# Two blocks in one kernel: one expert of 64 places to a bin with a floating 17th bin in the two later expert layers, and stage boundaries taken tile by tile

## The chip, the cores and the metric

The kernel runs on one core of one Trainium2 chip. The metric is the device time of one launch in microseconds (us), the median of several runs. PE is the matmul engine (TensorE), DVE the VectorE, ACT the ScalarE, POOL the GpSimd; SP issues nearly all the large transfers. All numbers are float32.

## What is computed

The reference is two blocks in a row on 256 tokens of width 1024. The first block has a mixer layer with a dense feed-forward part, then a convolution layer with 8 experts of which each token takes 2. The second block has two layers; each ends in 16 experts, of which a token takes 2 inside one group of 4:

```python
def grouped_moe(x, router_w, router_b, w_gate, w_up, w_down):
    ...
    scores = jax.nn.sigmoid(jnp.dot(xt.astype(jnp.float32), router_w.astype(jnp.float32)))
    sel = scores + router_b.astype(jnp.float32)
    group_score = lax.top_k(sel.reshape(-1, N_GROUPS, GROUP_SIZE), TOP_K)[0].sum(-1)
    top_group = jnp.argmax(group_score, axis=-1)
    ...
    for e in range(N_EXPERTS_2):
        h = jax.nn.silu(xt @ w_gate[e]) * (xt @ w_up[e])
        out = out + combine[:, e:e + 1] * (h @ w_down[e])
    return out.reshape(bsz, seq, d)
...
def second_block(...):
    for i in range(DEPTH):
        ...
        x = layer_norm(ALPHA * x + o, ln1_g[i], ln1_b[i])
        f = grouped_moe(x, router_w, router_b, w_gate[i], w_up[i], w_down[i])
        x = layer_norm(ALPHA * x + f, ln2_g[i], ln2_b[i])
```

Here d = 1024 and an expert is 512 wide, so the three weight matrices of one expert are 6.29 MB and those of one layer's 16 experts 100.7 MB. Between the stages of the first block stand updates `x + gate * rmsnorm(y)`, each followed by a new rmsnorm.

On the inputs that the reference draws, its own router gives the 16 experts of each later layer 5 to 67 tokens: expert 12 has 67 in both layers, the next fullest 55 and 56. The four groups have 47 to 82 tokens.

## The kernel before

The program is written by engine: each engine's stream is fixed in the source, and semaphores tie them. No scheduler reorders anything.

**Three expert stages.** They are objects of a class `Moe`: MOE1 (8 experts, 11 column steps of 256), MOEA and MOEB (the two later layers). A stage sorts tokens into bins of CAP = 96 places. In MOE1 a bin is one expert. In MOEA and MOEB a bin is one group of 4 experts, and the 96 places of the bin are sent through all 4 of its experts; the gate of an expert, zero for places that didn't choose it, is multiplied into the hidden values. A *block* is one column step of one expert: 2.1 MB of up weights (w1 and w3) and 1.05 MB of down weights. MOE1 has 88 blocks, MOEA and MOEB 32 each (16 experts by 2 steps).

**A round** on PE is `up(r)` (L1080): the array is used as four column strips of 32, each strip takes 32 places of some block, so a block of 96 places is three strips, a round four, and a stage has blocks x 3 / 4 rounds (24 in MOEA and MOEB). Each round is 32 matmuls; a float32 matmul shows as two records in the trace, so 64. Then come `turn_hidden` (L1092: two transposes), and `down` (L1108: 12 matmuls, 24 records, per block) for the blocks that were ended two rounds before. Per bin there is one `turn_places` (L1130) and four `scatter` matmuls (L1140), each added by DVE to TOK (L2433). Transposed places and scattered sums go through one PSUM bank, bank 3.

**Ahead of the rounds** the tokens are gathered into the bins by matmuls with one-hot matrices (L1053, one-hots made by DVE at L2365), and in MOEA and MOEB `slot_gates` (L1062) fetches the gates of the places. PE starts to gather once DVE has read the counts (memset of L2372, which frees the bank).

**Loads.** `expert_loads` on SP fills a ring of 4 slots (`ring`, one block's w1 and w3 each, L506) and one of 4 down slots (`dring`, L514). A slot is free when the round that used it is over. Up weights come in pieces of 256 columns, that is 1 KB in a row; down weights 4 KB in a row.

**Boundaries of stages.** `post` takes the statistics of a result (DVE, `bn_stats`), multiplies it by the gate vector GP, waits for ACT's square root (`root`), and updates X; `rms` takes the statistics of X, again a root, and `scale_rows` writes the normed tokens. PE then transposes all 16 pieces (`turn_job`, L777), and ACT copies them (L1440, L1442). Behind the second block's layers `layer_norm` (L1920) does both in one go. PE is given small jobs on the modulation weights to do meanwhile: lists FILL, GAP2 (four jobs before the dense part), GAP3, LATE, GAP4, GAP5. A job's columns are summed (L730), taken by ACT (`mod_parts`, L1471), and turned (L743, L746); DVE reads the outcome (L1992, L1997). For gated columns DVE also needs rows that POOL loads into the one buffer RB (`gate_rows`).

Of the kernel before, what the change touches and what calls it, by code (L numbers as in the profile page):

```python
# [7 lines left out]
P = 128  # L8
F32 = mybir.dt.float32
ALU = mybir.AluOpType  # L10
# [34 lines left out]
class Moe:  # L45
# [3 lines left out]
    def __init__(self, name, bins, experts, halves):  # L49
        self.name, self.bins, self.experts, self.halves = name, bins, experts, halves  # L50
        self.steps = experts * halves
        self.blocks = bins * self.steps
        self.rounds = self.blocks * 3 // 4
        self.before = {}

    def counts(self):

        n = {name: self.rounds for name in ("upped", "silued", "hidden", "turned_h", "hidden_turned")}
        n |= {name: KC * self.bins // 4 for name in ("gathered", "gather_taken")}
        n |= {name: self.bins for name in ("places_turned", "places_taken", "ys_ready", "slots_placed")}  # L60
        n |= {name: 4 * self.bins for name in ("scattered", "added")}
        n |= {name: int(self.experts > 1) for name in ("slot_gated", "slot_gates_taken", "mixed_gates")}
        n |= {"all_placed": TT, "down_done": self.blocks, "up_in": 32 * self.blocks // RING, "down_in": 16 * self.blocks // RING}
        return n

    def pieces(self, r):

        return [divmod(4 * r + g, 3) for g in range(4)]

    def home(self, i, c):  # L70

        return divmod(3 * i + c, 4)

    def done_in(self, i):

        return (3 * i + 2) // 4
# [8 lines left out]
    def starts(self, b):  # L85

        return 3 * b * self.steps // 4
# [3 lines left out]
MOE1 = Moe("1", NE1, 1, NSTEP)  # L91
MOEA = Moe("A", NG, GS, NSTEP2)
MOEB = Moe("B", NG, GS, NSTEP2)
# [46 lines left out]
GAP2 = ["mod0_10", "mod0_11", "mod1_3", "mod1_0"]  # L140
GAP3 = ["mod1_1", "mod1_2"]
# [3 lines left out]
GAP5 = ["mod1_10", "mod1_11"]  # L145
MODS = FILL + GAP2 + GAP3 + LATE + GAP4 + GAP5
# [47 lines left out]
def two_blocks(nc, A, out):  # L194
# [3 lines left out]
    with ExitStack() as ctx:  # L198
# [50 lines left out]
        chosen = sb("chosen", [P, TT, NE1])  # L249
        place = sb("place", [P, TT, NE1 + 1])  # L250
        sgt = sb("sgt", [P, NG, 3, GS])
        sgm = sb("sgm", [P, NG, 2])
# [3 lines left out]
        flag = sb("flag", [P, 4], mybir.dt.int32)  # L256
# [3 lines left out]

        dring = carve(dreg, 0, RING, 2, D)
# [25 lines left out]
        gG = H[0:GR, :, :].rearrange("p a n -> p (a n)")  # L287
        nM = HT[0:GR, 0, :, :].rearrange("p a n -> p (a n)")
# [11 lines left out]
        XGS = {"1": carve(wide, 2 * D, KC, NE1 * CAP), "A": carve(wide, D, KC, NG * CAP), "B": carve(wide, D, KC, NG * CAP)}  # L300
        XG2 = carve(wide, 2 * D, KC, P)
        PMG = arena[:, 4096:4096 + 1536]
        router_parts = H[:, 0, :]
# [3 lines left out]
        PTM = carve(T2f, D + 4 * P, 4, P)  # L307
        PM2 = carve(T2f, D, 2, P)
# [83 lines left out]
        def unrolled(m):  # L392
            return 1 if m is MOE1 else m.halves

# [7 lines left out]
        def second_pass(eng, m, first, steps, tail, end=False):  # L402
# [6 lines left out]
            with eng.If(spilled(eng, m) > 0):  # L409
                with eng.Fori(0, m.bins) as b:  # L410
# [7 lines left out]
                if end:  # L418
                    eng.wait_ge(sem(f"baton{m.name}"), 1 + 2 * m.bins * baton_bin(m))
# [3 lines left out]
        def _(sp):  # L423
# [66 lines left out]
            def expert_loads(m, w1, w3, w2, updated):  # L490


                def columns(i):
                    b, q = divmod(i, m.steps)
                    e, st = divmod(q, m.halves)
                    return b * m.experts + e, slice(st * FSTEP, (st + 1) * FSTEP)

                def up(i):
                    s = i % RING
                    e, f = columns(i)  # L500
                    if i < RING:
                        slot_free(s)
# [14 lines left out]
                for i in range(RING):  # L517
                    up(i)
# [2104 lines left out]
```

## Time and profile before

| | us |
|---|---|
| median of 3 runs | 2550.6 (2549.83 to 2553.07) |
| the profiled execution, its own time | 2545.95 |
| its span, first to last instruction | 2544.2 |
| PE busy | 2360.1 (93%) |
| DVE busy, ACT busy | 487.6 (19%), 366.0 (14%) |
| moved by DMA | 644.55 MB, mean 253 GB/s |

PE rows are records of pipelined matmuls: on four strips at once, 64 records of 0.59 us each take 7 us together. The idle time that a timeline row names stands before that row, with what ended it. "x" is a count. PEld are weight loads, which run beside matmuls.

### The profile page before, as it was taken

The numbers are of one execution on the slowest core, as the hardware profiler recorded it, in microseconds if no ns is written. First come the engines' busy times: TensorE is split into PE (matmuls) and PEld (weight loads), VectorE is DVE, ScalarE is ACT, GpSimd is POOL, SyncE is SP. The second block draws the span as 40 slices with busy tenths as digits, with TensorE's granted clock in tenths as the row PEclk, the third lists the DMA queues.
The fourth block names the chain that finished last, engine by engine and source line by source line (L and its number), as shares of the span: only waits on it lengthen the run. The fifth ranks groups of instructions, "written<-read, shape, count | busy, mean of one in ns | idle before, by whom it ended". The sixth has DMA issues, their size and how long they took to land. (4 is left out here: it accounts for less than half of the span.)

```text
span 2544.2 us, 34498 instructions
## 1 busy us (share of the span) xinstructions
PE 2360.1 (93%) x15206; PEld 1002.0 (39%) x15206; DVE 487.6 (19%) x1168; ACT 366.0 (14%) x868; POOL 33.0 (1%) x78
## 2 busy tenths in 40 slices
PE   4999989998999899999999999886999989799997
PEld 1574634443865332222223222253422227342222
DVE  2143830002094300000000000213100021310002
ACT  2023420001232210000000000121100011110000
POOL 2000000000000000000000000000000000000000
PEclk9999989999999999999999999997999999899999
DMA  8231286444354799999999999812899972479993
GB/s 292 77 122 66 100 286 228 152 141 176 117 207 166 265 316 351 366 364 367 364 366 366 363 364 367 287 64 99 293 364 364 359 274 76 129 244 364 365 359 145
DMA packets 446103, 644.55 MB, mean 253 GB/s; under 512 B 10723, under 2 KB 345019, under 8 KB 445947
## 3 DMA queue, kind: packets, MB, share of 16 engines
q1 hardware_dynamic: 442011, 629.55, 72.0%
q0 software_dynamic: 3936, 12.69, 1.5%
q8 instruction: 126, 2.06, 0.3%
q14 instruction: 30, 0.25, 0.0%
HBM read 641.15 MB, written 1.05 MB: 252 GB/s over the span
## 5 line engine op out<-in xcount | busy, mean ns | idle before, releaser
L1080 PE MATMUL bank<-ring,wide 128*32 128x512 f32 x7296 | 808.2, 595 | 1.7 <-ACT wide L1663 0.9
L1080 PEld LDWEIGHTS bank<-ring,wide 128*32 128x32 f32 x7296 | 231.8, 110 | 548.6 <-issue 548.5
L1108 PE MATMUL bank<-dreg,RB 128*32 128x512 f32 x3648 | 415.0, 595 | 0.0
L1670 ACT ACTIVATE SG<-bank 128x256 f32<-128x256 f32 x114 | 43.7, 383 | 1187.2 <-PE bank L1080 1187.2
L1108 PEld LDWEIGHTS bank<-dreg,RB 128*32 128x32 f32 x3648 | 106.8, 109 | 223.8 <-issue 223.8
L719 PE MATMUL bank<-wide,ring 128*128 128x256 f32 x832 | 182.1, 381 | 0.0
L719 PEld LDWEIGHTS bank<-wide,ring 128*128 128x128 f32 x832 | 158.9, 191 | 23.0 <-issue 1.4
L2409 DVE TENSOR_TENSOR H<-SG,bank 128x256 f32<-128x256 f32 x66 | 27.8, 421 | 717.3 <-ACT SG L1670 717.3
L1007 PE MATMUL bank<-ring,wide 128*128 128x512 f32 x352 | 156.2, 597 | 4.4 <-DVE MODX L1997 4.4
L709 PE MATMUL bank<-ring,wide 128*128 128x512 f32 x352 | 155.2, 599 | 1.0 <-DMA ring<-in_w_kv 1.0
L709 PE MATMUL bank<-ring,T 128*128 128x512 f32 x256 | 113.4, 603 | 1.4 <-ACT sm L1842 0.8
L709 PEld LDWEIGHTS bank<-ring,wide 128*128 128x128 f32 x352 | 67.2, 193 | 82.7 <-issue 81.1
L1007 PEld LDWEIGHTS bank<-ring,wide 128*128 128x128 f32 x352 | 65.9, 192 | 79.8 <-issue 75.0
L2414 DVE SCALAR_TENSOR_TENSOR H<-SG,sgt,bank 128x256 f32<-128x256 f32 x32 | 15.4, 481 | 339.7 <-ACT SG L1670 339.7
L1018 PE MATMUL bank<-dreg,HT 128*128 128x512 f32 x176 | 79.3, 593 | 1.0 <-ACT HT L1623 1.0
L709 PEld LDWEIGHTS bank<-ring,T 128*128 128x128 f32 x256 | 49.2, 194 | 62.5 <-issue 60.3
L1140 PE MATMUL bank<-T 128*128 128x512 f32 x128 | 69.5, 636 | 3.9 <-ACT T L1687 3.9
L2306 DVE SCALAR_TENSOR_TENSOR T<-dreg,PCOL,T 128x256 f32<-128x256 f32 x180 | 71.8, 481 | 0.1
L730 PE MATMUL bank<-ring,CB 128*32 128x512 f32 x384 | 50.3, 655 | 22.3 <-DMA ring<-in_l_mod_w 22.3
L1092 PEld LDWEIGHTS bank<-ident,H 128*128 128x128 f32 x228 | 23.0, 141 | 94.9 <-issue 94.9
L2433 DVE TENSOR_TENSOR TOK<-bank,TOK 128x512 f32<-128x512 f32 x64 | 43.9, 685 | 41.6 <-PE bank L1140 41.6
L2262 DVE TENSOR_TENSOR H<-SG,bank 128x256 f32<-128x256 f32 x22 | 9.2, 420 | 214.0 <-ACT SG L1616 214.0
(388 smaller groups left out, 1403.0 us busy)
## 6 DMA issues: line engine op xcount, KB each, us to landing
ring<-in_l_moe_w SPq DMA_DIRECT2D x176, 1024.0 KB, 11.5
dreg<-in_l_moe_w SPq DMA_DIRECT2D x88, 1024.0 KB, 12.4
ring<-in_w_gate SPq DMA_DIRECT2D x64, 1024.0 KB, 11.3
ring<-in_w_up SPq DMA_DIRECT2D x64, 1024.0 KB, 13.5
dreg<-in_w_down SPq DMA_DIRECT2D x64, 1024.0 KB, 12.2
ring<-in_l_mod_w SPq DMA_DIRECT2D x24, 2048.0 KB, 8.0
ring<-in_l_ffn_w SPq DMA_DIRECT2D x22, 1024.0 KB, 10.1
ring<-in_l_w_in SPq DMA_DIRECT2D x7, 2048.0 KB, 9.0
```

The lines of the kernel that those rows point to most:

```text
L709: m = pe.matmul(o[:, lo:lo + n], src[:, k, t * P:(t + 1) * P], w[:, k, 0:n], start=k == 0, stop=k == KC - 1)
L719: m = pe.matmul(o[:, i * T:(i + 1) * T], w[:, k, (2 * j + i) * P:(2 * j + i + 1) * P], src[:, k, :], start=k == 0, stop=k == KC - 1)
L730: m = pe.matmul(o[QUAD * g:QUAD * (g + 1), :], CQ[:, 4 * r + g, :], w[:, 4 * r + g, :], start=r == 0, stop=r == 1)
L1007: m = pe.matmul(banks[t][:, :], T1[:, k, t * P:(t + 1) * P], ring[:, s, k, :], start=k == 0, stop=k == KC - 1)
L1018: m = pe.matmul(banks[4 + 2 * t + n][:, :], HT[:, t, j, :], dring[:, s, j, n * NCH:(n + 1) * NCH], start=st == 0 and j == 0, stop=st == NS ...
L1080: mm = pe.matmul(banks[r % 2][32 * g:32 * g + 32, :], xg[:, k, at:at + 32], ring[:, i % RING, k, :], start=k == 0, stop=k == KC - 1)
L1108: return pe.matmul(banks[4 + 2 * (b % 2) + h][32 * g:32 * g + 32, :], HQ[:, r % 4, j, 32 * q:32 * q + 32], dring[:, i % RING, j, h * NCH:( ...
L1140: pe.matmul(o[:, :], PTM[:, 2 * h + t, :], YS[:, h * NCH:(h + 1) * NCH], start=True, stop=True).then_inc(sem("moe_scattered"), 1)
L1670: act.activation(SG[:, r % 2, :], banks[r % 2][:, 0:FSTEP], ACT.Silu).then_inc(sem("moe_silued"), 1)
L2306: dve.scalar_tensor_tensor(T2[:, k, :], hT[:, k, tap:tap + T], w, T2[:, k, :], ALU.mult, ALU.add).then_inc(sem("tap"), 1)
L2409: i = dve.tensor_tensor(H[:, r % 2, :], SG[:, r % 2, :], banks[r % 2][:, FSTEP:NCH], ALU.mult)
L2433: dve.tensor_tensor(v, o[:, :], v, ALU.add).then_inc(sem("moe_added"), 1)
```

## The change

**The later expert layers.** MOEA and MOEB get one bin of 64 places per expert and a 17th bin of 64 more, which takes the places 65 to 128 of whichever expert is fullest (`fullest_bin` on DVE; SP reads its number from `flag` and loads that expert's weights again). If anyone has more than that, the second pass runs, as it did for bins over 96. A block is now two strips, so a layer has 34 blocks and 17 rounds. `down` is 8 matmuls. Two bins make a unit that is turned and scattered together: 9 units, 36 scatters in place of 16. Gates are multiplied into the scatter matrix (`place_slots`), so `slot_gates` is gone. The tokens are gathered in quarters of four bins: 16 matmuls ahead of round 0, four in each of rounds 0 to 11, and 16 narrow ones for bin 17 in round 13. In these gathers the stationary operand takes every eighth column of X, since the weights' rows are now laid out as `(p k)`.

**Loads of all three expert stages.** Up weights are loaded as pairs of blocks, halved by rows: 2 KB in a row in MOE1, 8 KB in a row in MOEA and MOEB. The half `upped_low` frees its slot before the rest of the round.

**Boundaries.** ACT takes sums of squares (`squares`), a piece or a tile at a time, in place of DVE's statistics; DVE multiplies by the gate piece by piece; `update`, `norm_tokens` and `scale_rows` signal each of the two tiles, and `turn_job` turns tile 0 while tile 1 is made. On ACT the first root stands ahead of the modulation jobs. GAP2 has three jobs, GAP3 three in place of two. A second buffer RB2 takes every other set of gated rows from mod0_11 on. The output leaves in two transfers.

```diff
-        self.steps = experts * halves
-        self.blocks = bins * self.steps
-        self.rounds = self.blocks * 3 // 4
+        self.cap = 32 * chunks
+        self.bins = experts + (chunks == 2)
+        self.blocks = self.bins * steps
+        self.rounds = self.blocks * chunks // 4
...
-MOEA = Moe("A", NG, GS, NSTEP2)
+MOEA = Moe("A", NE2, NSTEP2, 2)
...
-GAP2 = ["mod0_10", "mod0_11", "mod1_3", "mod1_0"]
-GAP3 = ["mod1_1", "mod1_2"]
+GAP2 = ["mod0_10", "mod0_11", "mod1_0"]
+GAP3 = ["mod1_1", "mod1_2", "mod1_3"]
...
+                            for e, lo, n, at in m.runs(q):
+                                rows = w(expert(e)).rearrange("(k p) n -> p k n" if m is MOE1 else "(p k) n -> p k n", p=P)
+                                sp.dma_start(pairs[:, slot, i, :, at:at + n], rows[:, 4 * h:4 * h + 4, lo:lo + n]).then_inc(
...
+                def gather_quarter(n, o):
+                    q, pair = divmod(n, 4)
+                    upto("all_placed", TT * (q + 1))
+                    ks, w = (range(KC), 64) if q == 4 else (range(2 * pair, 2 * pair + 2), 4 * 64)
+                    for j, k in enumerate(ks):
+                        for t in range(TT):
+                            i = pe.matmul(o[:, j * w:(j + 1) * w], src[:, t, :].rearrange("p (d k) -> p k d", k=KC)[:, k, :],
+                                          PMQ[q % 2][:, t, 0:w], start=t == 0, stop=t == 1)
...
+                        if r < 12 or r == 13:
+                            if left:
+                                upto(*left)
+                            gather_quarter(gathered, banks[3])
...
+                        for i in m.ended(r - 2):
+                            down(i)
+                            if r >= 4 and r <= m.rounds:
+                                scatter_pair(scattered // 4, scattered % 4, banks[3], left)
...
+                        if (r % 2 == 1 and r >= 3) or r == m.rounds + 1:
+                            turn_places(turned, ("added", scattered) if r == m.rounds + 1 else left)
...
-            for f in GAP2:
+            root_of_pieces()
+            mod_parts(GAP2[0])
+            root_of_tiles(X, XN)
+            for f in GAP2[1:]:
                 mod_parts(f)
-            root()
-            root()
...
+                for t in range(TT):
+                    step(dve.scalar_tensor_tensor(src[:, t, :], src[:, t, :], mv[:, t, 0:1], g, ALU.subtract, ALU.mult))
+                    if t == 0:
+                        invert_root()
+                    m = dve.scalar_tensor_tensor(X[:, t, :], src[:, t, :], sm[:, 64 + t:65 + t], b, ALU.mult, ALU.add)
+                    m.then_inc(sem("x_tile"), 1)
```

On PE, from the router of MOEA on, before the change (arena holds the one-hots, ring and dreg the weights, RB the turned hidden values):

```order
L1298 MATMUL bank<-chosen,CB 128x4 x2
L1053 MATMUL bank<-arena,X 128x384 x16
L1062 MATMUL bank<-gates,arena 128x4 x24
L1080 MATMUL bank<-ring,wide 32x512 x64
L1092 MATMUL bank<-ident,H 128x128 x2
L1080 MATMUL bank<-ring,wide 32x512 x32
L1092 MATMUL bank<-ident,H 128x128 x2
```

and after it, from the same place and then the fourth round with scatters (L1117 gather, L1139 up, L1149 turn_hidden, L1166 down, L1216 scatter, L1196 turn_places):

```order
L1117 MATMUL bank<-arena,X 128x256 x16
...
L1139 MATMUL bank<-ring,wide 32x512 x32
L1149 MATMUL bank<-ident,H 128x128 x2
L1117 MATMUL bank<-arena,X 128x256 x4
L1166 MATMUL bank<-dreg,RB 32x512 x8
L1216 MATMUL bank<-T,XN 128x512
L1166 MATMUL bank<-dreg,RB 32x512 x8
L1216 MATMUL bank<-T,XN 128x512
L1196 MATMUL bank<-ident,T 128x128 x4
```

The work before round 0 is shorter, and gathers, scatters and turns stand in nearly every round, all through bank 3.

On ACT, at the end of the mixer (SG and CB take the modulation jobs' columns, sm the roots), before:

```order
L1598 ACTIVATE XN<-bank 128x512 x4
L1471 ACTIVATE SG<-bank 128x512
L1473 ACTIVATE sm<-sm 128x1
L1471 ACTIVATE CB<-bank 128x512
...
L1428 ACTIVATE sm<-sm 128x16 x2
```

and after:

```order
L1545 ACTIVATE SG,sm<-bank 128x512 x4
L1540 ACTIVATE sm<-sm 128x2
L1603 ACTIVATE SG<-bank 128x512
...
L1545 ACTIVATE XN,sm<-X 128x1024 x2
L1540 ACTIVATE sm<-sm 128x2
L1603 ACTIVATE CB<-bank 128x512
...
L1603 ACTIVATE SG<-bank 128x512
```

The roots, which stood behind all the jobs, now stand behind the squares and behind the first job; the later jobs wait for them.

## Rows read from the trace of the kernel before

**Rows 1.** The page's 40 slices of the span: GB/s moved.
```profile
GB/s 292 77 122 66 100 286 228 152 141 176 117 207 166 265 316 351 366 364 367 364 366 366 363 364 367 287 64 99 293 364 364 359 274 76 129 244 364 365 359 145
```

**Rows 2.** Windows: length, busy PE PEld DVE ACT POOL (x), PEclk, DMA share, GB/s.
```profile
42.00:55.00 13.00, 10.17 (x77) 5.92 (x70) 1.53 (x12) 5.52 (x12) 0.00 (x0) 1.00 1.05 387
2217.00:2226.00 9.00, 3.54 (x29) 2.28 (x27) 3.88 (x20) 3.47 (x9) 0.00 (x0) 0.88 1.10 348
2228.00:2236.00 8.00, 7.68 (x19) 4.43 (x20) 2.40 (x6) 1.96 (x4) 0.00 (x0) 0.76 1.03 410
1000.00:1600.00 600.00, 599.20 (x5188) 176.16 (x5180) 41.76 (x91) 48.06 (x126) 0.00 (x0) 1.00 1.07 365
2246.00:2514.00 268.00, 268.00 (x2315) 78.11 (x2315) 19.74 (x44) 21.37 (x56) 0.00 (x0) 0.99 0.97 330
```

**Rows 3.** Groups of PE in 2228.3 to 2530 (MOEB): xcount | busy, mean ns.
```profile
L1080 PE MATMUL bank<-ring,wide 128*32 128x512 f32 x1536 | 170.7, 597 | 0.0
L1108 PE MATMUL bank<-dreg,RB 128*32 128x512 f32 x768 | 87.4, 595 | 0.0
```

**Rows 4.** Chain of work, rounds of MOEB: start, us, what.
```profile
2362.07 7.00 PE bank L1080 x64
2369.08 0.37 PE bank L1092 x2
2369.45 2.71 PE bank L1108 x24
2372.16 1.06 PE bank L1140 x2
...
2391.73 5.29 PE bank L1108 x48
```

**Rows 5.** Timeline of PE: the start of MOEB, and a turn of places.
```profile
2228.32 12.27 PE L1053 MATMUL bank<-arena,X 128*128 128x384 f32 x32 [0.96 <-DVE sm L2372]
2240.43 5.67 PE L1062 MATMUL bank<-gates,arena 128*128 128x4 f32 x48
2246.03 15.31 PE L1080 MATMUL bank<-ring,wide 128*32 128x512 f32 x128
...
2518.74 0.63 PE L1130 MATMUL bank<-ident,T 128*128 128x128 f32 x4 [0.87 <-DVE TOK L2433]
```

**Rows 6.** The page's groups: a matmul of 256 columns; weight loads in MOEB (PEld).
```profile
L719 PE MATMUL bank<-wide,ring 128*128 128x256 f32 x832 | 182.1, 381 | 0.0
```
```profile
L1053 PEld LDWEIGHTS bank<-arena,X 128*128 128x128 f32 x32 | 6.8, 217 | 5.9 <-issue 2.1 <-DVE arena L2365 0.5
```

**Rows 7.** Timeline of PE: first work behind the boundaries, idle time before it.
```profile
375.68 1.12 PE L746 MATMUL bank<-ident,SG 128*128 128x128 f32 x4 [10.18 <-DVE wide L1992]
...
385.49 6.94 PE L1007 MATMUL bank<-ring,wide 128*128 128x512 f32 x12 [4.43 <-DVE MODX L1997]
...
635.10 3.68 PE L777 MATMUL bank<-ident,XN 128*128 128x128 f32 x16 [9.59 <-DVE XN L1942]
...
841.96 3.14 PE L777 MATMUL bank<-ident,XN 128*128 128x128 f32 x16 [1.92 <-DVE XN L1942]
...
1650.19 2.18 PE L777 MATMUL bank<-ident,X 128*128 128x128 f32 x9 [10.89 <-DVE X L1953]
...
1769.49 3.67 PE L777 MATMUL bank<-ident,X 128*128 128x128 f32 x16 [7.35 <-DVE X L1937]
```

**Rows 8.** Timeline of DVE: behind the mixer, and the last add of MOEB.
```profile
357.96 2.36 DVE L1949 TENSOR_TENSOR XN<-XN,wide 128x1024 f32<-128x1024 f32 x2
366.60 0.25 DVE L1891 RECIPROCAL sm<-sm 128x16 f32<-128x16 f32 x1 [6.28 <-ACT sm L1428]
...
369.40 2.47 DVE L1899 BATCH_NORM_STATS2 sm<-X 128x6 f32<-128x512 f32 x4
...
383.40 0.69 DVE L1992 TENSOR_TENSOR wide<-bank,RB 128x512 f32<-128x512 f32 x1 [7.06 <-DMA RB<-in_l_ffn_post_g]
...
2529.66 0.69 DVE L2433 TENSOR_TENSOR TOK<-bank,TOK 128x512 f32<-128x512 f32 x1 [0.17 <-PE bank L1140]
```

**Rows 9.** Timeline of ACT before MOE1: the tables for the root.
```profile
831.99 1.28 ACT L1428 ACT_TABLE_LOAD   x1
```

More of the change, by code:

```diff
@@ L54, in __init__ @@
         self.before = {}
     def counts(self):
[L58 to L62, printed above, removed]
@@ L85, in starts @@
     def starts(self, b):
-        return 3 * b * self.steps // 4
+        return self.chunks * b * self.steps // 4
 U_FFN = TT * NSTEP
-MOE1 = Moe("1", NE1, 1, NSTEP)
-MOEA = Moe("A", NG, GS, NSTEP2)
-MOEB = Moe("B", NG, GS, NSTEP2)
+MOE1 = Moe("1", NE1, NSTEP, 3)
+MOEA = Moe("A", NE2, NSTEP2, 2)
+MOEB = Moe("B", NE2, NSTEP2, 2)
 MOES = (MOE1, MOEA, MOEB)
@@ L392, in unrolled @@
         def unrolled(m):
-            return 1 if m is MOE1 else m.halves
+            return 1 if m is MOE1 else m.steps
         def baton_bin(m):
@@ L1075, in up @@
+                def up(r):
+                    if m is MOE1 and r in (0, m.starts(4)):
+                        upto("gather_taken", 2 * KC if r else KC)
+                    if m is not MOE1 and r % 4 == 0:
+                        upto("gather_taken", r + 4 if r < 16 else 17)
                     if r >= 2:
                         upto("hidden", r - 1)
-                    for k in range(KC):
-                        for g, (i, c) in enumerate(m.pieces(r)):
-                            at = CAP * (i // m.steps) + 32 * c
-                            mm = pe.matmul(banks[r % 2][32 * g:32 * g + 32, :], xg[:, k, at:at + 32], ring[:, i % RING, k, :],
-                                           start=k == 0, stop=k == KC - 1)
@@ L1802, in _ @@
             moe(MOE1, SCL[:, 4, :], MODX[:, 1, 24:32])
-            root()
+            act.wait_ge(sem("tokens_summed"), 1)
+            for t in range(TT):
+                squares(YS, TOK[:, t, :], tile_sums[:, t:t + 1])
+            act.wait_ge(sem("squared"), cnt["squared"])
+            root_of_sums(tile_sums)
+            cnt["tiles"] += 1
             operand(T1)
@@ L2438, in moe @@
                         multiply(r)
+                    if m is not MOE1:
+                        if 4 <= r <= m.rounds:
+                            for p in range(2):
+                                add(r // 2 - 2, 2 * (r % 2) + p, banks[3])
+                        if r == m.rounds + 1:
+                            for p in range(4):
+                                add(final - 1, p, banks[p])
+                        if r >= 2 and r % 2 == 0 and r < m.rounds:
+                            place_slots(r // 2 - 1)
+                        if r == m.rounds:
+                            place_slots(final)
+                        if r in (3, 7, 11):
+                            one_hots(m, 2 + r // 4)
+                        continue
                     for b in range(m.bins):
@@ L2483, in _ @@
             moe(MOE1)
-            post(1, TOK)
+            step(dve.memset(sm[:, 446:447], 0.0), "tokens_summed")
+            for t in range(TT):
+                m = dve.tensor_tensor(XN[:, t, :], TOK[:, t, :], GP[:, 1, :], ALU.mult)
+            step(m)
+            update(XN)
             dve.wait_ge(sem("gelu_done"), 1)
```

693 lines of the change are left out of this document (431 added, 262 removed).

## The prediction

> **What bounds the kernel now.** I first read the 40 slices [rows 1]: the transfers run at about 365 GB/s through slices 17 to 24 and again through the middle of MOEA and MOEB, and are slack elsewhere. That looks like a bound by DMA. The windows say otherwise [rows 2]: in 1000 to 1600 (MOE1) PE is busy 599.2 of 600 us, and in 2246 to 2514 (MOEB) 268.0 of 268, with no wait for a load in it. So in the expert stages PE sets the end, and DMA just keeps up with it: the two are within a few per cent of each other. This is what the reader is to keep in mind, for the change takes work from PE there and gives more to DMA. Between stages nobody is busy but a chain of small steps on DVE and ACT: PE's idle times before its first work are 10.18 and 4.43 us behind the mixer, 9.59 behind the dense part, 1.92 before MOE1, 10.89 behind it, 7.35 before each later expert stage [rows 7].
>
> **Which price an operation has.** A record in four strips of 512 columns costs 7.00 / 64 = 0.109 us in the chain [rows 4] (0.597 long, but four at once [rows 3]). A block's down is 5.29 - 2.71 = 2.58 us for 24 records, 1.72 for the new 16. A scatter costs 1.06, and the next step in strips 0.13 more (2.71 for 2.58) [rows 4]: 1.19. A full-array record of 256 columns costs 182.1 / 832 = 0.219 [rows 6].
>
> **The later expert layers, per layer.** Before, the rounds run from 2246.03 to the last scatter, read by DVE at 2529.66 [rows 5, 8]: 283.6 us for 24 rounds. After, 17 rounds:
> - rounds 0 and 1: up and turn 7.37, a gather of 8 records 1.75, and 0.3 for going out of strips and back: 9.4 each, 18.8;
> - rounds 2 and 3: two downs more, one turn of places: 26.6;
> - rounds 4 to 11: 7.37 + 2.05 + 3.44 + two scatters 2.38 = 15.3; every second one also turns places 0.63 and has to wait for the add of the last scatter, which before cost 0.87 [rows 5]: 16.8. Together 128.4;
> - rounds 12 to 16: 13.3 each, two turns with their waits 3.0, bin 17's gather of 32 narrow records at 5.67 / 48 = 0.118 [rows 5]: 4.1 with the switch. 73.6;
> - tail: 7.9 for round 17; the last turn, downs and eight scatters 13.9 (10.9 before, less 1.7 for shorter downs, and four scatters and their wait more).
>
> The sum is 269.2, so 14.4 less, though the rounds fell by 7: scatters (36 for 16) and the gathers that now stand inside give back most of it. The way to round 0 took 17.7 us (12.27 gather, 5.67 slot gates, overlapping slightly [rows 5]). It becomes 32 records, 7.0 us, about 1.5 more since the clock stands at half there (0.76 mean granted in 2228 to 2236 [rows 2]), and 0.8 for ACT's last copy. It starts 1.5 later: DVE frees the counts' bank only behind four one-hots and four small steps in place of one one-hot (the gather waited for exactly that memset [rows 5]). Hence 10.8, which is 6.9 less. Other new steps of `fullest_bin` lie under the gather. Per layer 21.3, for two layers **-42.6**.
>
> **Do the loads hold?** From the restart of the stream (half of round 0 over) to the up weights of round 16, 15 pairs of 4.19 MB and 24 downs of 1.05 MB must land: 88.1 MB. PE reaches round 16 some 229 us later. I need 385 GB/s. The rate depends on how much lies in a row: where only 1 KB pieces move (2217 to 2226) it is 348 GB/s, with 2 KB pieces 387, with 4 KB pieces 410 [rows 2]. The mix of the old rounds (two thirds at 348, a third at 410) is the 366 of rows 1. The new up weights have 8 KB in a row, the nearest row is 410: 215 us, 14 to spare. So I take no wait. At 366 the stage would be 12 us longer, at 348 24 us. In MOE1 the pieces grow to 2 KB, which loosens a tie that PE already won: 0.
>
> The Trainium skill (DMA: Bandwidth & Descriptors, Specifications) gives a limit of about 358 GB/s from HBM per core and calls pieces of 512 B enough for the full rate. By it the layer would be bound by DMA, some 17 us longer, 34 for both. This trace speaks against it: 387 and 410 GB/s stand in it, and 1 KB is slower than 4 KB [rows 2].
>
> **Behind the mixer.** The wait has two parts. DVE had its statistics before 357.96, but ACT's root came behind four modulation jobs (6.28 us idle [rows 8]), then statistics of X took 2.47 us more; and the gated rows of mod0_11 came late through the one buffer (7.06 us [rows 8]), so the dense part began at 385.49. After: last gate multiply 356.4, squares 357.1, root 357.6, X by 360.4, its squares on ACT 361.7, normed 363.8; PE is through its three jobs at about 364.8 (the second and third wait for ACT behind the squares), turns till 366.7, DVE has read the jobs at 367. PE starts at about 367.5: **-18**. The dense part's first up weights, issued when the first job frees its slot (358), are there at 366 by 348 GB/s, its first down weights at 385, needed at 388.
> **Behind the dense part:** ACT reads tile 0's sums early; 1.5 us of pieces, then 1.28 for the root's tables (as in [rows 9]) which now stand behind the squares, and the rest as above: turn at about 630 for 635.1. **-5**, with the third job inside the wait.
> **Before MOE1** the idle time was only 1.92 us, since the unit kv1v1 stood behind the jobs and covered the chain. Now the second job's columns are taken behind ACT's squares of X, at about 835.4, and PE is there at 832: it stands 3.4 us in front of kv1v1 instead, less the 1.92: **+1.5**.
> **Behind MOE1:** no statistics (2.5), squares 2.2 in their place beside the multiply, the tables exposed; 2 us, and half the turn hidden 2: **-4**.
> **Four layer norms:** the same DVE steps, but eight of 16 transposes (3.67 for 16 [rows 7]) run beside tile 1: 1.8 each for three, 0.7 for the store: **-6.1**.
>
> **Sum:** -42.6 - 18 - 5 + 1.5 - 4 - 6.1 = -74.2. The profiled execution took 2545.95 us, which gives 2471.8; against the median of 2550.6 it is **2476**.
>
> **Rivals.**
> 1. *DMA becomes the bound.* Larger pieces don't go faster: at 366 GB/s two layers lose 24 us: 2500; at 348 it is 2524. For it: DMA was at its edge already, and a layer moves 6.3 MB more. Against: 410.
> 2. *Bank 3 and the boundaries return less.* Gather, scatter and turn now pass through one bank in each round. Each hand-over has a down (1.72 us) before the next use, against 0.69 + 0.17 for an add [rows 8], so only the turn waits. If half of the some 40 hand-overs per layer cost 0.5 us, or the boundary behind the mixer yields half, it is 10 to 20 us: 2486 to 2496.
> 3. *Slower: the stationary loads of the gathers.* They read every eighth column. No such load is in the trace; those in a row last 0.217 and hide under 0.219 of matmul [rows 6], with no room. Bounds: at nothing, 0; the price decides from 0.19 us more per record, since 192 records a layer times that, twice, are 74 us. At twice 0.219 the time is 2476 + 2 x 45 = 2566. I take nothing, since most of the 0.217 is latency if matmuls of 0.109 hide loads of 0.11 as they do in the rounds, and nothing shows that the rate itself is at its limit.
>    The Trainium skill (SBUF — State Buffer, Door 1: The DMA port swizzle) says that each access which leaves a line of 16 bytes pays a penalty; a step of 32 bytes always does. It gives no price; it is why this rival has a chance at all.
> 4. *Second pass.* If two experts of a layer had over 64 tokens, 64 passes of 3.1 MB, one after another, would add at least 64 x 7.7 = 490 us at 410 GB/s. The reference's inputs have one such expert (67), so only a different draw would do it.
>
> **How the numbers follow.** Forecast, 2458 to 2490: 0.63. Rival 1, 2490 to 2524: 0.13. Rival 2 beyond 2490: 0.12. Rival 3 in part (2500 to 2545): 0.05, in full: 0.04. Rival 4: 0.02. The rest, 0.01, is a time within 0.2%. The range of 2455 to 2508 leaves out the upper half of rival 1, rival 3 and 4, about 0.17 with what may lie below. Faster by over 0.2% (what a measurement of this kernel can tell from none): 0.93; within: 0.01; slower: 0.06.
>
> **What would show it.** In the profile after: rounds of MOEB at 15 to 17 us with scatter and gather, 13.3 later on; no row in which `up` waits for a DMA; a rate near 400 GB/s with gaps, not a flat one; PE's wait behind the mixer under 3 us; a new one of 3 us before kv1v1. Wrong: an `up` that waits for ring<-in_w_gate in every round (rival 1); gather records over 0.25 us apart (rival 3); idle before scatters (rival 2).

## The result, and the profile after

| | us |
|---|---|
| before, median of 4 runs | 2550.7 (2549.83 to 2553.07) |
| after, median of 4 runs | **2490.2** (2487.45 to 2494.44) |
| ratio, 95% interval | 0.9763 (0.9746 to 0.978) |
| profiled execution after: own time, span | 2490.25, 2488.5 |
| PE busy after | 2311.2 (93%) |
| moved by DMA after | 657.00 MB, mean 264 GB/s |

The change gained 60.5 us where I had forecast 74.2; 2490.2 lies in the range of 2455 to 2508, at the upper edge of what I had called my forecast (2458 to 2490). The profiled executions, from which everything below is read, are 55.7 us apart and not 60.5, because the one before the change was 4.7 us faster than its median.

**The transfers.** The 40 slices of the page (clock in tenths, then GB/s), to be laid beside [rows 1]:

```profile
PEclk8999999999999999999999999998899999899998
GB/s 299 68 113 64 128 216 274 152 118 162 197 216 169 243 315 369 354 363 377 363 365 375 357 365 373 311 142 2 401 417 415 356 294 85 72 346 417 414 355 137
```

In MOEA and MOEB the rate is 414 to 417 where it was 364. The waits of PE have no `up` behind a DMA there. Windows in round 13 of MOEA, and one over rounds of MOEB (columns as in [rows 2]):

```profile
1965.00:1970.00 5.00, 5.00 (x28) 4.29 (x20) 0.42 (x1) 0.72 (x2) 0.00 (x0) 1.00 1.04 424
1970.00:1974.00 4.00, 4.00 (x20) 3.78 (x24) 0.00 (x0) 0.20 (x1) 0.00 (x0) 0.62 1.00 416
1970.00:1978.00 8.00, 8.00 (x33) 4.68 (x34) 0.00 (x0) 0.60 (x1) 0.00 (x0) 0.57 0.76 316
2260.00:2400.00 140.00, 136.50 (x992) 51.55 (x984) 22.02 (x51) 17.43 (x37) 0.00 (x0) 1.00 1.01 412
```

**The rounds** came as forecast but for one. Rounds 0 and 1 take 9.22 and 9.39 us, rounds 4 to 11 take 15.21 and 16.72 by turns, round 12 takes 13.19. Round 13, in which the places of bin 17 are gathered, takes 24.25 (24.53 in MOEB), not 18.9. Timeline of PE, rounds 13 and the start of 14 in MOEA:

```profile
1958.71 7.07 PE L1139 MATMUL bank<-ring,wide 128*32 128x512 f32 x64
1965.71 0.44 PE L1149 MATMUL bank<-ident,H 128*128 128x128 f32 x2
1965.99 7.78 PE L1117 MATMUL bank<-arena,X 128*128 128x64 f32 x32
1973.70 3.64 PE L1166 MATMUL bank<-dreg,RB 128*32 128x512 f32 x16
1977.27 1.35 PE L1216 MATMUL bank<-T 128*128 128x512 f32 x2
1978.55 1.92 PE L1166 MATMUL bank<-dreg,RB 128*32 128x512 f32 x16
1980.40 1.12 PE L1216 MATMUL bank<-T 128*128 128x512 f32 x2
1982.41 0.63 PE L1196 MATMUL bank<-ident,T 128*128 128x128 f32 x4 [0.88 <-DVE TOK L2667]
```

Two things are to be seen. The 32 narrow records of L1117 are 0.24 us apart, not the 0.118 of [rows 5]. And the down behind them takes 3.64 where the next one takes 1.92: the granted clock is 1.00 in 1965 to 1970, 0.62 in 1970 to 1974 and 0.57 in 1970 to 1978 (1.00 is 2.4 GHz, the lower of its two levels 1.2). So it fell while the narrow records ran, and PE had not been idle ahead of it. The weight loads of these gathers, by form, 1780 to 2000 (ns least/middle/most):

```profile
L1117 PEld LDWEIGHTS bank<-arena,X x128: 312/337/338, 1779.8 to 1973.2; 128*128 128x128 f32 x128
```

A load that takes every eighth column lasts 337 ns. The 217 of [rows 6] for neighbouring columns is a mean over both levels of the clock. Of the same loads in the kernel before, those in 2228 to 2232 (granted clock 0.53) and those in 2234 to 2241 (1.00):

```profile
L1053 PEld LDWEIGHTS bank<-arena,X x7: 258/338/338, 2228.3 to 2231.7; 128*128 128x128 f32 x7
L1053 PEld LDWEIGHTS bank<-arena,X x19: 190/190/190, 2234.0 to 2239.8; 128*128 128x128 f32 x19
```

So at the full clock it is 337 against 190. At the lower one the strided loads take no longer than the others: nine of them in 1762 to 1766 of the changed kernel, at 0.50, have a median of 340.

**Behind the mixer** the wait in front of the dense part is down to 0.89 us, and a new one stands behind its first steps, for the first down weights. **Before MOE1** stands the wait that I had forecast. Timelines of PE, to be laid beside [rows 7]; the last three rows are the turns behind MOE1 and ahead of MOEA:

```profile
372.21 13.97 PE L1064 MATMUL bank<-ring,wide 128*128 128x512 f32 x32 [0.89 <-ACT wide L1574]
...
399.03 6.26 PE L1075 MATMUL bank<-dreg,HT 128*128 128x512 f32 x8 [5.76 <-DMA dreg<-in_l_ffn_w]
...
816.17 1.10 PE L789 MATMUL bank<-CB 128*128 128x512 f32 x2 [3.33 <-issue]
817.10 8.73 PE L755 MATMUL bank<-ring,wide 128*128 128x512 f32 x16
...
1630.30 3.68 PE L831 MATMUL bank<-ident,X 128*128 128x128 f32 x16 [8.06 <-DVE X L2150]
...
1745.64 1.97 PE L831 MATMUL bank<-ident,X 128*128 128x128 f32 x8 [4.96 <-DVE X L2107]
1748.16 1.97 PE L831 MATMUL bank<-ident,X 128*128 128x128 f32 x8 [0.55 <-DVE X L2107]
```

**The account**, from the two profiled executions, by marks that both have (PE's or DVE's first or last record of a stage):

| stretch | forecast | before | after | difference |
|---|---|---|---|---|
| start to the end of wo | 0 | 355.6 | 360.3 | +4.8 |
| to the fourth unit of the dense part | -18 | 56.0 | 45.0 | -11.0 |
| dense part | 0 | 208.6 | 208.6 | 0 |
| behind it | -5 | 18.4 | 12.3 | -6.0 |
| convolution layer | 0 | 188.9 | 181.3 | **-7.6** |
| before MOE1, with its gather | +1.5 | 38.8 | 43.1 | +4.3 |
| MOE1 | 0 | 773.2 | 771.6 | -1.6 |
| behind MOE1 | -4 | 14.3 | 11.5 | -2.8 |
| MOEA and MOEB | -42.6 | 605.1 | 570.5 | -34.6 |
| the layers' other work, and the end | -6.1 | 285.4 | 284.3 | -1.1 |
| span | -74.2 | 2544.2 | 2488.5 | -55.7 |

### The profile page after: what moved, and what is told of

Same layout as the page of the kernel before. It is cut to its first block and busy times, and to the rows that moved or that the text cites. A ratio compares the mean times of both kernels' runs of the same rounds, so it can differ in the third digit from the quotient of the medians.

```text
span 2488.5 us, 32512 instructions
## 1 busy us (share of the span) xinstructions
PE 2311.2 (93%) x14114; PEld 1019.6 (41%) x14114; DVE 506.2 (20%) x1246; ACT 398.8 (16%) x919; POOL 33.6 (1%) x78
## 2 busy tenths in 40 slices
DMA packets 252000, 657.00 MB, mean 264 GB/s; under 512 B 11187, under 2 KB 50571, under 8 KB 234443
## 3 DMA queue, kind: packets, MB, share of 16 engines
q8 instruction: 117, 1.92, 0.3%
## 5 line engine op out<-in xcount | busy, mean ns | idle before, releaser
L1139 PE MATMUL bank<-ring,wide 128*32 128x512 f32 x6400 | 706.8, 593 | 2.1 <-ACT wide L1798 1.4
L1139 PEld LDWEIGHTS bank<-ring,wide 128*32 128x32 f32 x6400 | 200.2, 110 | 475.7 <-issue 472.4
L1166 PE MATMUL bank<-dreg,RB 128*32 128x512 f32 x3200 | 373.3, 601 | 0.0
L2644 DVE TENSOR_TENSOR H<-SG,bank 128x256 f32<-128x256 f32 x100 | 42.1, 421 | 994.5 <-ACT SG L1805 994.5
L1805 ACT ACTIVATE SG<-bank 128x256 f32<-128x256 f32 x100 | 38.4, 384 | 986.5 <-PE bank L1139 986.5
L1166 PEld LDWEIGHTS bank<-dreg,RB 128*32 128x32 f32 x3200 | 91.2, 110 | 204.8 <-issue 204.6
L2667 DVE TENSOR_TENSOR TOK<-bank,TOK 128x512 f32<-128x512 f32 x104 | 71.3, 689 | 209.3 <-PE bank L1216 196.4
L1117 PE MATMUL bank<-arena,X 128*128 128x256 f32 (+1 forms) x320 | 87.4, 426 | 4.2 <-DVE sm L2606 4.2
L1117 PEld LDWEIGHTS bank<-arena,X 128*128 128x128 f32 x320 | 80.4, 335 | 7.5 <-issue 6.1
L1075 PEld LDWEIGHTS bank<-dreg,HT 128*128 128x128 f32 x176 | 34.1, 195 | 50.4 <-issue 43.1
L1149 PEld LDWEIGHTS bank<-ident,H 128*128 128x128 f32 x200 | 20.3, 141 | 83.2 <-issue 83.2
```

Source lines behind the costliest of these rows:

```text
L1075: m = pe.matmul(banks[4 + 2 * t + n][:, :], HT[:, t, j, :], dring[:, s, j, n * NCH:(n + 1) * NCH], start=st == 0 and j == 0, stop=st == NS ...
L1117: i = pe.matmul(o[:, j * w:(j + 1) * w], src[:, t, :].rearrange("p (d k) -> p k d", k=KC)[:, k, :], PMQ[q % 2][:, t, 0:w], start=t == 0, s ...
L1139: mm = pe.matmul(banks[r % 2][32 * g:32 * g + 32, :].rearrange("p (w n) -> p w n", w=2), x, w, start=k == 0, stop=k == KC - 1)
L1166: return pe.matmul(banks[4 + 2 * (unit % 2) + h][32 * g:32 * g + 32, :], HQ[:, r % 4, j, 32 * q:32 * q + 32], dring[:, i % RING, j, h * NC ...
L1805: act.activation(SG[:, r % 2, :], banks[r % 2][:, 0:FSTEP], ACT.Silu).then_inc(sem("moe_silued"), 1)
L2644: i = dve.tensor_tensor(H[:, r % 2, :], SG[:, r % 2, :], banks[r % 2][:, FSTEP:NCH], ALU.mult)
```

## Experiments

All start from the changed kernel; each ratio is to the kernel before. Steps are read in the traces, since the medians of one kernel vary by some 2 us; the changed kernel itself gave 2491.8 us (2490.96 to 2495.3) in a second set of runs, beside the last two experiments.

### 1. Neighbouring columns, rows of 2 KB

```diff
-rows = w(expert(e)).rearrange("(k p) n -> p k n" if m is MOE1 else "(p k) n -> p k n", p=P)
+rows = w(expert(e)).rearrange("(k p) n -> p k n", p=P)
...
-i = pe.matmul(o[...], src[:, t, :].rearrange("p (d k) -> p k d", k=KC)[:, k, :],
+i = pe.matmul(o[...], src[:, t, k * P:(k + 1) * P],
```

> From the changed kernel (2490.2 us), in MOEA and MOEB only: the rows of the up weights are laid out as (k p) again, so a piece of a load is 2 KB in place of 8 KB, and the gathers take 128 neighbouring columns of X as stationary operand in place of every eighth. Everything is still computed. Theory P (the strided stationary load sets the pace of the gathers, 0.239 us a record; a row of 2 KB moves at 387 GB/s, as in 42 to 55 of the trace of before): the 32 narrow records of round 13 fall from 7.8 us to 3.8 and the granted clock does not fall behind them (1.7 to 2.7 us more), the 96 records within rounds 0 to 11 fall from 0.239 to 0.219 (1.9), the 32 ahead of round 0 by some 0.6. Together 8 to 9 us a layer. The loads then need about 388 GB/s between the middle of round 0 and round 16 (now 376), which is just what 2 KB rows gave: waits of 0 to 2 us a layer. Time 2472 to 2478. Rival T (the rate is that of the mix in the old rounds, 366 GB/s): 88.1 MB take 241 us where PE would take 227, so waits of 14 us a layer eat the gain: about 2500. Rival C (the narrow records are slow for another reason than the stride, such as the hand-over of bank 3): the gathers stay as they are, 2490 or more.

Measured: **2470.0 us** (2467.09 to 2473.02), ratio 0.9682 (0.9665 to 0.97). PE in round 13, PE's weight loads, and the window of MOEB:

```profile
1963.68 3.68 PE L1117 MATMUL bank<-arena,X 128*128 128x64 f32 x32
1967.29 1.92 PE L1166 MATMUL bank<-dreg,RB 128*32 128x512 f32 x16
```
```profile
L1117 PEld LDWEIGHTS bank<-arena,X x128: 186/190/192, 1781.0 to 1967.0; 128*128 128x128 f32 x128
```
```profile
2260.00:2400.00 140.00, 135.62 (x1016) 47.35 (x1018) 21.25 (x47) 19.27 (x40) 0.00 (x0) 1.00 1.04 394
```

The narrow records cost 0.115 us each, the down behind them 1.92, and round 13 takes 18.22 us. Rounds 0 to 11 are 0.29 shorter each. From the first `up` to that of round 16 it is 228.7 and 228.5 us, in place of 238.1 and 238.3. The whole stages are 9.6 and 10.5 us shorter, a little more than the 8 to 9 expected, and the time stands 2 us under the range. Theory P holds, rival C is out. The loads had to bring 88.1 MB in 225 us, 391 GB/s, and moved 394: one wait of 1.01 us in MOEA, none over 1 us in MOEB. So rival T, with its 366, is out too; but the rate is only 3 GB/s above what PE needs.

### 2. Neighbouring columns in MOEB alone, loads as they were

```diff
+(src[:, t, k * P:(k + 1) * P] if m is MOEB else
 src[:, t, :].rearrange("p (d k) -> p k d", k=KC)[:, k, :])
```

> From the changed kernel, in MOEB only: the gathers take 128 neighbouring columns of X as stationary operand, with the loads left as they are, so MOEB works on features in the wrong order and the last layer's output isn't the reference's; all the work is kept, and MOEA stands beside it unchanged. Theory P: narrow records 0.118 us apart in MOEB against 0.24 in MOEA, wide ones 0.219 against 0.239, round 13 of MOEB 18 to 19 us against 24.3 in MOEA, 8 to 9 us less for MOEB, 2482. Rival C (not the stride): round 13 is 24 us in both layers, 2490.

Measured: 2482.7 us (one run). Round 13 takes 24.20 us in MOEA and 18.22 in MOEB, rounds 0 to 11 of MOEB are 0.29 shorter. With the loads unchanged, the stride costs 9.5 us between the first `up` and that of round 16, with what the clock loses behind the narrow records counted in.

### 3. Rows of 1 KB

```diff
-return [(a, lo, 2 * FSTEP, 0)] if a == b else [...]
+return [(a, lo, 2 * FSTEP, 0)] if a == b and self.chunks == 3 else [...]
```

This stands on top of the edit of experiment 1.

> As the kernel with 2 KB rows, but each load of up weights in MOEA and MOEB is cut into two of 256 columns, so that 1 KB lies in a row; everything is still computed. Theory P (the rate goes by the bytes in a row: 348 GB/s at 1 KB and 410 at 4 KB in the trace of before): 62.9 MB of up weights at 348 and 25.2 MB of down weights at 410 take 242 us where PE would take 227, so 15 us of waits for up weights in each layer: 30 us more than the kernel with 2 KB rows if that one doesn't wait, about 2505, and within 1.5% of the changed kernel, so that most of the worth of the long rows is 15 us net. Rival S (the rate doesn't depend on the row from 512 bytes up, as the Trainium skill has it in DMA: Bandwidth & Descriptors, Specifications): same time as the kernel with 2 KB rows, within 3 us.

Measured: **2509.1 us** (2507.37 to 2509.72), ratio 0.9839 (0.9822 to 0.9855). PE's waits from 1780 to 2480, and the window of MOEB:

```profile
PE bank L1139 <- DMA ring<-in_w_up: 31.4, 24, 2.6
```
```profile
2260.00:2400.00 140.00, 129.80 (x936) 42.97 (x928) 19.89 (x45) 18.02 (x38) 0.00 (x0) 0.99 1.08 366
```

The rate is back at the 366 of the kernel before, `up` waits 24 times, and the time is 39 us over that of experiment 1, not 30. Between the stages of experiment 1 and these it is 21.0 and 17.6 us. Rival S falls; theory P has the direction and was a quarter low in the size (30 us for 39). The edit also halves each load (512 KB for 1,024, and twice as many), and no run separates the two. Against the size of the loads speaks the kernel before: its up weights came in loads of 1,024 KB with 1 KB in a row, and moved at 365 GB/s as well, with the engines' share at 1.07 [rows 2]. With 1 KB in a row the new layers would have been bound by DMA. What the Trainium skill states (DMA: Bandwidth & Descriptors, Specifications), full rate from 512 bytes up and some 358 GB/s at most, disagrees with these three windows: 366, 394 and 412 GB/s for up weights in rows of 1, 2 and 8 KB. (With 8 KB no `up` waited for a load, so 412 need not be the most that such rows can give.)

### 4. POOL's loads later

```diff
 pool.wait_ge(sem("x_updated"), 1)
+pool.wait_ge(sem("upped"), 8)
 pool.dma_start(TOK[:, :, :], A["mem_2"][0]...)
```

> From the changed kernel: POOL's loads of the memory tokens and of three rows of parameters (2.6 MB), which it issues when X is updated behind the mixer, now wait until eight units of the dense part are through. Theory Q (these loads run in front of the dense part's first up and down weights and make PE wait 5.76 us for the first down weights, and the granted clock's half behind that wait costs 2.7 us more): the wait at 399 us goes or falls under 1 us, 6 to 8.5 us less: 2482 to 2484. Rival R (the first down weights are late because SP issues them behind four up loads in 1 KB rows, whatever POOL does): the wait stays near 5 us, 2490.

Measured: **2482.5 us** (2481.89 to 2484.1), ratio 0.9735 (0.9719 to 0.9751). Timeline of PE at the same place:

```profile
385.21 7.03 PE L1065 MATMUL bank<-ring,wide 128*128 128x512 f32 x16
392.08 3.60 PE L1076 MATMUL bank<-dreg,HT 128*128 128x512 f32 x8
```

The wait of 5.76 us is gone, and the first down takes 3.60 in place of 6.26. Theory Q holds, in size too.

### 5. One buffer for the gated rows

```diff
-ROW_HOME = [0, 0, 0, 1, 0, 1, 0, 1]
+ROW_HOME = [0, 0, 0, 0, 0, 0, 0, 0]
```

> From the changed kernel (2490.2 us): the second buffer for the rows of gated columns is not used; all sets go through RB, each load issued when DVE has used the set before. Theory U (the buffer carries a part of the gain at the boundary behind the mixer, and the 7.6 us that the convolution layer gained without my having forecast it, since there PE had waited 5.3 us for DVE to read a gated job): the rows of mod0_11 land 4 to 7 us later, so the dense part starts 3 to 7 us later; the wait of 5.3 us in the convolution layer is back. 2498 to 2502. Rival V (the convolution layer gained by the third job of GAP3 and the sums of squares): only the first of the two, 2493 to 2497.

Measured: **2498.8 us** (2497.8 to 2502.32), ratio 0.9804 (0.9786 to 0.9823). Timeline of DVE at both places, then of PE:

```profile
379.17 0.69 DVE L2191 TENSOR_TENSOR wide<-bank,RB 128x512 f32<-128x512 f32 x1 [7.05 <-DMA RB<-in_l_ffn_post_g]
...
701.10 0.69 DVE L2191 TENSOR_TENSOR wide<-bank,RB 128x512 f32<-128x512 f32 x1 [5.12 <-DMA RB<-in_l_mix_post_g]
```
```profile
381.00 3.75 PE L1064 MATMUL bank<-ring,wide 128*128 128x512 f32 x4 [7.90 <-issue]
...
701.85 29.27 PE L1353 MATMUL bank<-dreg,XN 128*128 128x256 f32 x124 [4.71 <-DVE wide L2191]
```

and in the changed kernel, where the last one stands:

```profile
694.52 26.94 PE L1353 MATMUL bank<-dreg,XN 128*128 128x256 f32 x124
```

Behind the mixer DVE waits 7.05 us, as it did before the change (7.06 [rows 8]), and PE 7.90 in place of 0.89. The dense part starts 7.0 us later than in the changed kernel, counted from the end of wo. But at its fourth unit only 0.7 us of that is left (45.7 us for 45.0): PE has no wait for the first down weights here, where it waited 5.76 us in the changed kernel. In the convolution layer PE's wait of 4.71 is back, and the 124 records behind it take 29.27 for 26.94, with the granted clock at 0.66 in 697 to 707 (1.00 at this place in the changed kernel). That layer takes 188.6 us for 181.3. Theory U holds, but with its shares the other way round: the second buffer makes 7.3 of the 7.6 us in the convolution layer, and behind the mixer 0.7 us net, since the late down weights swallow what it brings there. Together 8.0, and the medians differ by 8.6.

### 6. The root last before MOE1

```diff
 mod_parts(GAP5[0])
-root_of_tiles(X, XN)
 mod_parts(GAP5[1])
+root_of_tiles(X, XN)
```

> From the changed kernel: before MOE1, ACT takes the columns of the second modulation job ahead of the squares of X and the second root, as it did in the kernel before, in place of behind them. Theory W (the new wait of 3.33 us in front of this job's turn, and the granted clock's half behind it, which stretches kv1v1 from 7.03 to 8.73, come from this order): the wait goes and kv1v1 is back at about 7.0; the chain to the normed tokens ends up to 1.3 us later and is covered by kv1v1 but for 0 to 2 us. 2 to 5 us less, 2485 to 2488. Rival Y (DVE's update of X sets the end of this boundary in either order): 0 to 1 us less, the idle time only moves behind kv1v1.

Measured: **2484.3 us** (2483.23 to 2486.53), ratio 0.9749 (0.973 to 0.9769). Timeline of PE:

```profile
812.17 1.02 PE L789 MATMUL bank<-CB 128*128 128x512 f32 x2
813.03 7.03 PE L755 MATMUL bank<-ring,wide 128*128 128x512 f32 x16
819.90 1.91 PE L831 MATMUL bank<-ident,XN 128*128 128x128 f32 x16
```

The wait is gone, kv1v1 is back at 7.03, and PE goes straight on to the turn: the tokens are normed by the time kv1v1 ends. The stretch before MOE1 takes 38.1 us, not 43.1. Theory W holds, and the chain behind costs nothing; my 2 to 5 us were a little low.

### 7. The second turn at the start in one piece

```diff
-turn_normed(TOK, 2)
+turn_whole(TOK, 2)
...
+for b in range(4):
+    if turn[0]:
+        pe.wait_ge(sem("turned_read"), 4 * (turn[0] - 1) + b + 1)
+    for j in range(2):
+        for t in range(TT):
```

> From the changed kernel: the second transposition at the start of the program (the context tokens) goes bank by bank with both tiles, as in the kernel before, in place of tile by tile. Theory Z (with both tiles ready and the banks coming free one by one, going by tiles holds every copy of ACT back until the second tile; it delays the first product of the mixer by 2.6 us and the clock's half behind it costs 1.7 more): 3 to 4.5 us less from about 58 us on, 2486 to 2487. Rival N (the later start is the launch and the first loads, not the order): less than 1 us.

Measured: 2491.4 us (2484.03 to 2492.99), ratio 0.977 (0.9745 to 0.9796): no difference that the times show. Timeline of PE, this kernel, and then the changed kernel:

```profile
50.65 0.63 PE L844 MATMUL bank<-ident,TOK 128*128 128x128 f32 x4 [2.14 <-ACT wide L1586]
...
54.21 10.23 PE L755 MATMUL bank<-ring,wide 128*128 128x512 f32 x21
```
```profile
53.01 0.41 PE L831 MATMUL bank<-ident,TOK 128*128 128x128 f32 x2 [2.13 <-ACT wide L1574]
...
57.50 6.73 PE L755 MATMUL bank<-ring,wide 128*128 128x512 f32 x13
```

From the turn to the first product it is 3.56 us in place of 4.49: 0.9 us, not 3 to 4.5. The clock's half behind it comes in either order: 0.88 granted in 54 to 64 here, 0.83 in the changed kernel, 1.00 in the kernel before. Theory Z had the right place and about a third of the 2.6 us of delay, and nothing of it in the times.

### 8. The counts' bank freed first

```diff
 if m is not MOE1:
+    o = take(f"cnt{m.name}")
+    step(dve.tensor_copy(sm[:, 336:336 + nb], o[:, 0:nb]))
+    free(dve.memset(junk, 0.0), f"cnt{m.name}")
     one_hots(m, 0)
```

> From the changed kernel, in MOEA and MOEB: DVE copies the counts of the bins and frees their bank before it makes the one-hots, not behind four of them and four small steps of fullest_bin. Theory B (PE's waits of 2.2 and 2.0 us before the first gather are for that bank): the waits fall to between 0.5 and 1.5 us, up(0) comes 1 to 1.5 us earlier in each layer, 2487 to 2489. Rival O (the first gather waits for the one-hots themselves): waits as before, 2490.

Measured: 2492.4 us (2491.78 to 2493.47), ratio 0.9782 (0.9763 to 0.9801). Timeline of PE:

```profile
1763.34 9.66 PE L1117 MATMUL bank<-arena,X 128*128 128x256 f32 x32 [1.35 <-DVE arena L2593]
```

The wait falls from 2.21 to 1.35 and now ends with the one-hots, as theory B has it. From the end of the router's matmuls to up(0) it is 0.6 us less in MOEA and 1.0 in MOEB, too little for the times, which don't reach the 2487 to 2489 expected.

### 9. Bin 17 gathered in four lots

```diff
-if r < 12 or r == 13:
+if r < 16:
     gather_quarter(gathered, banks[3])
...
-ks, w = (range(KC), 64) if q == 4 else (range(2 * pair, 2 * pair + 2), 4 * 64)
+ks, w = range(2 * pair, 2 * pair + 2), 64 if q == 4 else 4 * 64
```

> From the changed kernel: the gather of the 17th bin goes in four lots of eight narrow records in rounds 12 to 15, in place of 32 records in round 13; the stationary operand stays strided. Theory D (the granted clock falls to half behind the burst of 32 narrow records, 6.8 us long in each layer, and costs 1.7 to 2.7 us, while a record costs 0.24 us wherever it stands): no fall of the clock between rounds 12 and 16, four lots of about 2.2 us with the switch in and out of strips, together 0.5 to 1 us more than in one; the layer is 1 to 2 us shorter, 2486 to 2489. Rival E (the lots bring three more hand-overs of bank 3 on to the path): 2 to 4 us more, 2492 to 2494.

Measured: **2486.4 us** (2485.28 to 2488.61), ratio 0.9748 (0.9732 to 0.9763). PE, one lot and what follows it; the window of rounds 12 to 15 of MOEA in this kernel, then in the changed one:

```profile
1957.58 2.01 PE L1117 MATMUL bank<-arena,X 128*128 128x64 f32 x8
1959.52 1.93 PE L1166 MATMUL bank<-dreg,RB 128*32 128x512 f32 x16
```
```profile
1940.00:2016.00 76.00, 73.37 (x530) 27.89 (x526) 11.33 (x25) 10.38 (x24) 0.00 (x0) 1.00 0.90 358
```
```profile
1940.00:2016.00 76.00, 73.37 (x524) 26.34 (x524) 10.91 (x24) 8.54 (x18) 0.00 (x0) 0.96 0.85 333
```

The clock stays at 1.00, a record still costs 0.24, and rounds 12 to 15 take 63.2 us in both layers in place of 65.3 and 65.6. Theory D holds: of what round 13 lost, some 2 us are the clock (the down and the scatters behind the burst take 2.0 us more than the next ones), the rest is the stride. Rival E is out.

### 10. All of it together

The edits of experiments 1, 4, 6, 7 and 8.

> All the edits together that moved time down or were meant to: 2 KB rows with neighbouring columns in the gathers, POOL's loads behind eight units of the dense part, the second job's columns ahead of the root before MOE1, the second transposition at the start by banks, and the counts' bank freed first. Theory F (the places are apart from each other and the gains add): 2470.0 less 7.7, 5.9, 0.9 and 1.6: 2454, between 2450 and 2458; rounds of MOEA and MOEB as in the kernel with 2 KB rows. Rival G (a gain at one boundary is given back, since loads that start earlier meet others, or the later stage starts before its weights are there): over 2460.

Measured: **2456.9 us** (2453.52 to 2458.45, 5 runs), ratio 0.9629 (0.9614 to 0.9643); the changed kernel beside it gave 2491.8, ratio 0.9775 (0.976 to 0.9789). That is 35 us less, and everything is still computed. Theory F holds; PE has no wait over 1.1 us for a load in MOEA and MOEB.

Of the changed kernel's second set of runs I had expected:

> The changed kernel itself once more, beside the others on the same chip: 2488 to 2492, so that the steps of 1 to 8 us are read against it and not against a run on another chip.

## Why the prediction was right, and where its steps were off

**Right: what bounds the layers, and the way a round is put together.** The loads held, and the rate did rise with the length of the rows. Experiment 3 shows that this had to be so: rival 1 was real and was kept off by the longer rows, of which 2 KB are enough. I had priced it at 12 us a layer for 366 GB/s; between experiments 1 and 3 it is 21.0 and 17.6, since PE had less to do than I thought.

**Right by luck in part: the size.** Rounds 0 to 12 of the changed kernel hit within 0.2 us each, but with the stride in them. Without it rounds 0 to 11 are 0.29 shorter, so my terms for a round were about as much too high as the stride was dear. Without the stride MOEA and MOEB gain 54.7 us and not 42.6 (34.6 and the 20.1 of experiment 1); with it the two errors cancel down to 8. The whole is put together in the same way: 2490.2 would be some 2498 without the 7.6 us of the convolution layer, which I had at 0, and these stand against misses of 7 behind the mixer, 5 at the start, 5 in the layer norms and 3 before MOE1. That experiment 1 stands at 2470, near my 2476, is such a sum too.

**Wrong: "I take nothing" for the strided loads.** I argued that most of the 0.217 us of a load is latency, so that a stride would not show. But the 0.217 was a mean over both levels of the clock (190 ns at the full one), and the stride lengthens the load itself, to 337 ns. With such loads 0.24 us a record is the pace, twice that of a narrow record. The wide ones lose little (0.29 us a round of eight), since their 0.219 nearly covers it; the narrow ones lose 4.1 us, and the clock behind them 2 more. My term for bin 17 was 4.1 us; it measured 9.5 in the changed kernel, and 3.5 without the stride. Both layers together lose 19 us. So a part of rival 3 came true. Its full price was also worked out wrong: a layer has 160 such records (the trace has 320 loads for both), not 192, which by the same working makes it 77 us and not 90, and the 19 a quarter of it. And my sign for it, records over 0.25 us apart, would have missed it at 0.24. The Trainium skill (SBUF — State Buffer, Door 1: The DMA port swizzle) gives the rule, a penalty for each access that leaves a line of 16 bytes; the trace agrees with it at the full clock and gives the price: 337 for 190 ns.

**Behind the mixer: right up to the dense part's first matmul, wrong behind it.** I had PE start at 367.5; less the later start of 4.75 it starts at 367.46. But "its first down weights at 385, needed at 388" counted SP's queue alone. The step of X that releases the turn also releases four loads of POOL, 2.6 MB, and these moved ahead with it. Of the forecast 18 us, 7 went there (experiment 4 returns 7.7). What the second buffer brought to this place was hidden by the same wait (experiment 5). I had taken into the sum each queue that an edit names, and not the queue that waits on the same semaphore.

**Before MOE1:** the wait of 3.4 us came as 3.33, yet the stretch lost 4.3 and not 1.5. I had left out that the clock falls behind such a wait (8.73 for 7.03), and I had set against it the old 1.92, which the faster chain would have removed anyway (experiment 6).

**The convolution layer** gained 7.6 us that I had at 0. RB2 stood in my list of what is changed; I asked what it does behind the mixer and not where else DVE reads gated rows. Experiment 5 gives 7.3 us of it back: 4.7 of PE's wait, and 2.3 of the 124 records behind it, which began at the lower clock.

**The start** lost 4.8. The first product of the mixer begins at 57.50 for 54.91. In the profiles of the other kernels with this start it begins anywhere from 55.59 (experiment 1) to 59.53 (experiment 9), by how long PE waits for the first loads; so up to 1.9 us belong to this one execution, and 0.9 is the turn by tiles (experiment 7). From there to the end of wo it takes 302.8 us for 300.7. These 2.1 go with the clock: 0.83 granted in 54 to 64 for 1.00, and in experiment 10, where it is 1.00, the stretch takes 301.1. Why it falls there is open.

**The layer norms** should have given 6.1 us and gave 1.1. The turns themselves did what I wrote: to the end of the transpositions the four places gained about 1.2 to 1.6 each. Between MOEA and MOEB it was given back: the same 64 records of woB take 30.33 us where they took 27.73, the 256 records ahead of them 56.52 where they took 55.42, and the granted clock in the stretch is 0.81 in place of 0.86. Before, and then after:

```profile
2155.00:2228.00 73.00, 49.21 (x156) 28.32 (x156) 23.49 (x64) 15.27 (x41) 0.00 (x0) 0.86 0.38 122
```
```profile
2116.00:2190.00 74.00, 51.31 (x152) 27.72 (x150) 23.30 (x65) 14.85 (x39) 0.00 (x0) 0.81 0.34 132
```

The same stretch stands at 0.80 and 0.81 in the profiles of experiments 4 and 9 and of the changed kernel's second set, so the lower clock is not that of one execution. But it isn't bound to the new boundaries either: in experiment 3, which has them all, woB takes 27.73 again, with the clock at 1.00 in its first 10 us. What brings it about is open.

**Rival 2** (bank 3) did not happen: turns wait 0.88 us as before (0.87 [rows 5]), scatters within the rounds not at all.

## What to carry to other kernels

When a layout is changed so that transfers get longer pieces, look at what it does to the operands on chip, and take only as much length as the bound asks for: here 8 KB rows cost 19 us on PE for a rate (412 GB/s) that nobody needed; the 394 of 2 KB rows were just enough. When a step is moved forward, list everyone who waits on its semaphore, on all queues, and put their loads in front of yours in the sum. And a buffer that is doubled for one place is to be looked up at every place that uses it; the same edit gave 0.7 us net where it was expected, since another wait stood behind it, and 7.3 where nobody had looked.

## What the runs showed of the hardware

- At the full clock a float32 load of 128 stationary columns takes 186 to 192 ns if they are neighbours and about 337 if every eighth is taken; at the lower level both take about 340. With the strided loads records of matmuls came 0.24 us apart at the full clock, with 64 moving columns as with 256.
- The granted clock fell within 7.8 us of narrow matmuls on strided loads though PE was never idle (1.00, then 0.62 and 0.53 in the 4 us from 1966, 1970 and 1974). It stayed at 1.00 where the same matmuls, on loads of neighbouring columns, took 3.7 us (experiment 1), and where they went in four lots (experiment 9).
- The DMA rate over 140 us of an expert stage was 366, 394 and 412 GB/s with up weights in rows of 1, 2 and 8 KB (the first in loads of half the size; with the last PE, not DMA, was the bound).
